# Alternating differential and forgetting units in the row-maximum stage of a hybrid attention step

## The reference, cut to what matters

```python
s = jnp.einsum('bqmhd,bkmhd->bmhqk', q, k) * (DH_A ** -0.5)      # branch A
s = jnp.where(dist >= 0, s - slopes[:, None, None] * dist, NEG_INF)
p = jax.nn.softmax(s, axis=-1)
p = p[:, 0] - lam * p[:, 1]
...
s = jnp.einsum('bqhd,bkhd->bhqk', q, k) * (DH_B ** -0.5)         # branch B
s = s + F_q - F_k
p = jax.nn.softmax(jnp.where(q_pos >= k_pos, s, NEG_INF), axis=-1)
...
y = (jax.nn.sigmoid(m_a) * y_a + jax.nn.sigmoid(m_b) * y_b) @ w_o
```

## Time and profile before

| | |
|---|---|
| median of 3 runs | 2641.86 us |
| lowest, highest run | 2637.68 us, 3716.84 us |
| profiled execution | 2647.03 us, span 2645.1 us |
| PE busy over the span | 2516.0 us, 95% |
| DVE busy | 1594.3 us, 60% |
| ACT busy | 907.6 us, 34% |
| mean granted TensorE clock | 0.978 |

### The profile page before, as it was taken

One profiled execution on the slowest core, in us unless ns is written; L12 is line 12 of the kernel. 1 busy time (PEld: TensorE's weight loads), 2 busy tenths in 40 slices (PEclk: granted clock), 3 DMA queues, 4 the chain that ended last, 5 costly groups with the idle time before them and its releaser, 6 DMA issues. The chain is left out here.

```text
span 2645.1 us, 33588 instructions
## 1 busy us (share of the span) xinstructions
PE 2516.0 (95%) x12315; PEld 1994.8 (75%) x12315; DVE 1594.3 (60%) x2615; ACT 907.6 (34%) x1421; POOL 190.3 (7%) x182
## 2 busy tenths in 40 slices
PE   5899999997999989999999899999999897999998
PEld 2688888885788768888888687877777654788886
DVE  3321234657346637787887488877878655655554
ACT  4011112234222327885001465644444332322221
POOL 0000000222012220000000200000000000000000
PEclk8999999999999989999999899999999998999999
DMA  8463645644455367674445966435557297543431
GB/s 293 159 238 145 234 146 168 202 154 133 158 164 168 93 172 189 156 184 127 135 133 139 197 153 144 93 79 112 106 115 161 63 326 254 174 128 127 143 117 64
DMA packets 285838, 413.00 MB, mean 156 GB/s; under 512 B 77707, under 2 KB 169451, under 8 KB 276140
## 3 DMA queue, kind: packets, MB, share of 16 engines
q1 hardware_dynamic: 275242, 379.36, 50.4%
q10 hardware_dynamic: 9404, 31.73, 3.3%
q0 software_dynamic: 1056, 0.13, 0.1%
HBM read 273.62 MB, written 137.52 MB: 155 GB/s over the span
## 5 line engine op out<-in xcount | busy, mean ns | idle before, releaser
L1667 DVE CUSTOM_DVE_ANT_0 max_s_ps<-max_s_ps,max_causal 128x128 f32<-128x128 f32 (+7 forms) x256 | 194.6, 768 | 80.7 <-PE max_s_ps L1735 55.4
L704 PE MATMUL proj_z<-first_km,h_hi 128*128 128x512 f32 x576 | 228.8, 397 | 0.0
L704 PE MATMUL proj_z<-first_km,h_lo 128*128 128x512 f32 x576 | 226.1, 392 | 0.0
L704 PE MATMUL proj_z<-first_v,h_hi 128*128 128x512 f32 x576 | 224.1, 389 | 0.0
L2060 ACT ACTIVATE att_b_pf<-att_b_s_ps 128x1024 f32<-128x1024 f32 (+2 forms) x160 | 142.7, 898 | 113.2 <-PE att_b_s_ps L2117 88.2
L1626 ACT ACTIVATE max_s_ps<-max_s_ps,max_neg_top 128x128 f32<-128x128 f32 (+2 forms) x192 | 161.2, 839 | 43.1 <-DVE max_neg_top L1667 30.4
L2077 DVE TENSOR_TENSOR att_b_p_lo<-att_b_pf,att_b_p_hi 128x1024 fp32r<-128x1024 f32 (+2 forms) x160 | 170.5, 1066 | 5.5
L1670 DVE TENSOR_REDUCE max_neg_top<-max_s_ps 128x1 f32<-128x1024 f32 x128 | 156.1, 1225 | 23.1 <-PE max_s_ps L1735 12.3
L704 PE MATMUL proj_z<-proj_w_hi,h_hi 128*128 128x512 f32 x384 | 151.2, 394 | 0.0
L704 PE MATMUL proj_z<-proj_w_hi,h_lo 128*128 128x512 f32 x384 | 149.8, 390 | 0.0
L704 PE MATMUL proj_z<-proj_w_lo,h_hi 128*128 128x512 f32 x384 | 149.5, 389 | 0.0
(11 more groups left out here) (453 smaller groups left out, 6232.5 us busy)
## 6 DMA issues: line engine op xcount, KB each, us to landing
w_raw<-in_w_in SPq DMA_DIRECT2D x144, 256.0 KB, 5.1
smp_v_a<-scratch_mixes SPq DMA_DIRECT2D x16, 1024.0 KB, 4.9
map_qm<-scratch_q_hi SPq DMA_DIRECT2D x48, 256.0 KB
map_k<-scratch_k_hi SPq DMA_DIRECT2D x37, 256.0 KB
head_w<-in_w_ada SPq DMA_DIRECT2D x8, 1024.0 KB, 7.7
scratch_mixes<-proj_out SPq DMA_DIRECT2D x32, 256.0 KB, 2.2
scratch_v_hi<-proj_v_hi SPq DMA_DIRECT2D x32, 256.0 KB, 2.1
scratch_v_lo<-proj_v_lo SPq DMA_DIRECT2D x32, 256.0 KB, 2.5
```

The lines of the kernel that those rows point to most:

```text
L704: ins = nc.tensor.matmul(out, left(*lt), right(*rt), start=first and n == 0, stop=last and n == len(terms) - 1)
L1667: nc.vector.tensor_tensor_reduce(s, s, causal[:, 1024 - w:1024], -1.0, -NEG, ALU.add, ALU.min, accum_out=neg_top[:, kh, u, qt:qt + 1]).the ...
```

## The change

The units are taken in turn, one of A and one of B: before 0, 4, 1, 5, 2, 6, 3, 7, 8, 9, ... 15, now 0, 8, 4, 9, 1, 10, 5, 11, 2, 12, 6, 13, 3, 14, 7, 15. Everything that told A tasks from B tasks by position (`NTA`) now looks at a list `summed`, and the count that PE waits for in `sum_done` is taken from a running count, `sums_before`. The planner is run again over the new sequence with the same costs.

```diff
-UNITS = [m * HA + h for h in range(HA) for m in range(2)] + list(range(2 * HA, NU))
+UNITS = [u for h in range(HA) for m in range(2) for u in (m * HA + h, 2 * HA + 2 * h + m)]
...
-    NTA = NA * PER
+    summed = [u < NA for _, u, _, _, _ in tasks]
+    sums_before = [sum(summed[:n + 1]) for n in range(NT_)]
...
-    pe_us = [(2 if n < NTA else 1) * (w / 2400 + 0.02) for n, w in enumerate(width)]
+    pe_us = [(2 if summed[n] else 1) * (w / 2400 + 0.02) for n, w in enumerate(width)]
...
-    act_us = [0.43 + w * 0.84e-3 if n < NTA else 0.0 for n, w in enumerate(width)]
+    act_us = [0.43 + w * 0.84e-3 if summed[n] else 0.0 for n, w in enumerate(width)]
...
-    q_need = [sum(64 if y // 2 < NA else 32 for y in range(x % RING, x + 1, RING)) for x in range(2 * NU)]
+    q_need = [sum(64 if UNITS[y // 2] < NA else 32 for y in range(x % RING, x + 1, RING)) for x in range(2 * NU)]
...
-                    while x < min(upto[n], NTA):
-                        total(x)
+                    while x < upto[n]:
+                        if summed[x]:
+                            total(x)
...
-                        dve.wait_ge(sum_done, NTA)
+                        dve.wait_ge(sum_done, NA * PER)
...
-                        if y < NTA:
-                            pe.wait_ge(sum_done, y + 1)
+                        if summed[y]:
+                            pe.wait_ge(sum_done, sums_before[y])
```

## The result

The changed kernel takes 2650.35 us in the median of 7 runs (2645.06 to 2655.39), the kernel before 2640.64. The ratio is 1.0033, with a 95% interval of 1.0019 to 1.0047: 8.7 us more, 5.0 to 12.4. By the bound of 2% that is no change, but it is a loss, and six times the 1.4 us that the prediction gave it. The one run of before at 3716.84 us, far from all others, is left out of the ratio.

A forecast was written before the change was run, and what follows sets the result against it. TensorE, busy nearly throughout the joint stage with 1.6 us of waiting to win back, was taken as the bound. Waits of 3.0 us come and 1.6 go: 2641.9 + 1.4 = 2643.3 us, range 2634 to 2653.

The forecast's parts named there:

- the case within 2%: Whole kernel: the time changes by no more than about 2%, 53 us, either way; chance 0.95.
- the bounds of what was priced: Joint stage: from minus 1.6 us (all three detours absorbed, 2640.3) to plus 4.3 (each costs its whole 1.98, 2646.2).
- Queues that are moved past: ACT's and SP's queues in the joint stage: late copies, stores and query and key loads cost 0 us.
- The waits for exponentials: Joint stage: TensorE waits for late exponentials behind sampled tiles 8, 26 and 44: 1.2, 0.8 and 1.0 us, together 3.0.
- What goes: Joint stage: the second sampled tile's wait goes as it falls into a B unit, 0.64 us; the first's 0.97 is repriced.
- The sum: Whole kernel: 3.0 us of waits come and 1.6 go, plus 1.4 us, so 2643.3 us; chance 0.75.
- The signs of being wrong: Joint stage: wrong if PE waits for a load, a unit's first scores start late, or matmuls stay over 0.23 us apart.
- Absorbed: Rival, joint stage: ACT's even load absorbs the detours and no exponential is late, 2640.3 us; chance 0.15.
- The clock falls: Rival, joint stage: each of three new waits brings 13 slow matmuls, 2.6 us, giving 2651.1 us; chance 0.05.
- The loads come late: Rival, each unit's first task: PE waits for query and key loads, 5 us at 14 starts, 2712 us; chance 0.03.
- Pace: Joint stage: A and B units take about as long as each other before and after, so 0 us.

The follow-up runs named there:

- after_again: The changed kernel unedited, run again for a second trace ("the second trace"), against the kernel before: ratio 1.0033.
- direct_sum: The changed kernel, but DVE writes a sampled tile's sum straight to the output buffer and ACT only does the move: ratio 1.0013 to the kernel before.
- shifted: The changed kernel with the alternation shifted by one unit (A, A, B, A, B, ... B, B), same planner: ratio 1.0003 to the kernel before.
- before_late: The kernel before, all A units first, with every row block of the gate weights issued one tile later: ratio 1.0072 to the kernel before.
- hold_loads: The changed kernel, but SP issues no query or key loads in a sampled tile, they wait for the next tile: ratio 1.0029 to the kernel before.

## Why the time fell in the range and the larger wait was missed

**The time and the sign.** 2650.35 us lies in the range of 2634 to 2653, and the case within 2% came, but the forecast of 2643.3 is 7 us short, and the bounds of what was priced ended at 2646.2. That the range held is in part luck: it was stretched by the spread of single executions and 2 us more, and this room took in a wait that nothing in the sum stood for. The term that was missing is in *Queues that are moved past*. It priced one kind of SP's DMAs, the query and key loads, by their lead of 21 us, and wrote zero. The gate weights go through the same queue behind those loads. Their lead was in no row of the prediction, though the listing of the loop shows it: a chunk's last row block is issued in tile 7 (of 0 to 8), so two tiles are all that covers it. The same part worked out how short a tile can be, 5.3 us, but held only ACT's copy against it and not the weights. In the profiled execution this cost 4.6 us by starts, and in the second trace 4.2 and 1.5 more where the clock fell. It also priced a 256 KB DMA at the median of 4.4 us; the weights that were late took 7.4 and 9.0.

**The waits for exponentials.** Places and mechanism were right. The sizes were 1.2, 0.8 and 1.0 us, 3.0 together; measured are 1.3, 1.0 and 0.55, 2.9 together; the third was sized by tile 8 of before, which is followed by a task of 128, where tile 44 is followed by one of 384; whether that halves it was not tested. The argument that ACT's rest in the B units does not help was right too: ACT is at 45% and still late, because the detour and the slack are both within 5 us. `direct_sum` took the detour away and the waits went.

**What goes.** The wait behind tile 17 went, and the B units' sampled tiles cost nothing, as forecast.

**The sum.** In the profiled stage 2.9 and 4.6 us come and 1.6 go, 5.9. From the 25th product matmul on the stage is 6.3 us longer, in the second trace 7.5, with the clock's 1.5. The runs say 8.7, 5.0 to 12.4. What is left, 1 to 2 us, is within the interval and was not followed.

**The signs of being wrong.** The prediction said that it is wrong if PE waits for a load. PE did, for the gate weights, so by its own sign the account was wrong in this part. The stage was also to keep its length within some 3 us and grew by 5.0 and 7.6, and the clock was to stay at 1.00 and did so in one trace of two.

**The rivals.** *Absorbed* did not come. *The clock falls* was right as a mechanism and wrong in its place: not behind the waits for exponentials, up to 1.3 us, but behind one for weights of 3.1, in one trace of two. *The loads come late* named the queue and the wait correctly, but for `max_q` and `max_k`, of which none was late; it was set to decide at a lead of 21 us, and the weights, with 4 and 7, had passed their own point.

**Pace.** Units of one length held, and with it came the side that was not foreseen: where units keep their length, tiles change theirs. A tile is 24 matmuls and whatever scores fall in it, so ahead of chunk 2 two of them went from 22.5 us to 13.3.

What stays open is why, at leads of 6.8 to 7.0 us and full DMA engines in each, the weights of chunk 4 were late in the changed kernel and those of chunks 1 and 3 in the shifted one and of chunk 4 in `direct_sum` were not. Below 5 us behind an A half unit's loads every start waited, from 9.5 us on none did; between them these traces go either way. Whether the loads that follow have a part in it is not shown.

## What to carry to other kernels

When a plan moves work between the steps of a loop, list every DMA that is issued a fixed number of steps ahead of its use, and work its lead out again in microseconds from the shortest steps. Hold it against the time that such a DMA takes behind everything the queue carries at that place, 6 to 9 us here, and not against its median of 4.4. The transfer with the shortest lead goes first in its queue; that single edit gave back 7.7 of the 8.7 us here. Evening out an engine's load bought nothing here, where its lateness comes from one dependency that crosses two engines.

## What the runs showed of the hardware

After TensorE's waits of up to 2.3 us within this stage (the longest of these in `direct_sum`) the granted clock stayed at 1.00, and matmuls of 512 columns went on 0.22 to 0.24 us from start to start once the first was through. After waits of 2.9 to 6.3 us by starts the clock was at its lower level in five of six cases (after_again, three of before_late, and hold_loads, there only from 1.3 us after work had resumed), and stayed at full in one, the 3.0 us in the first trace of the changed kernel. At the stage's own start, behind an idle time of 5.1 us, the number of slow matmuls differed between traces, from 7 to 14. Weights of 256 KB were in place within 3.5 us of their issue at a DMA share of 0.60, and 7.4 to 9.0 us after it in the changed kernel, at 1.03 to 1.05, behind an A half unit's loads; in `shifted`, at 1.05 and behind the same loads, they landed after 6.1 us. The rest of the kernel, which no edit touched, took between 2145.4 and 2155.1 us in eleven traces, so a change of 5 us in one stage has to be read from that stage and from many runs, and not from two spans.
